# A split index projection and a three-block first product in a two-block transformer kernel

## The reference

```
for l in 0, 1:
    h    = rmsnorm(x) * g
    proj = h @ w_in[l]       # q,k,v of A, B, C (512 columns each), q_idx 256, k_idx 64, w_idx 4, gates 3072
    q_B, k_B, q_C, k_C, q_idx, k_idx = rope(...)
    A    = band attention;  B = differential attention
    C    = attention over the 64 keys that score highest by
           sum_h w_idx[q,h] * relu(q_idx[q,h] . k_idx)
    x   += (sum of gated up-projections of A, B, C) @ w_out[l]     # "out", two halves of 512 columns
    x   += cross attention over 256 memory tokens
    x   += (silu(h2 @ w_g) * (h2 @ w_u)) @ w_down                  # "gate_up" in 11 pieces, "down" in 22 chunks
```

## Time and profile before

| what | value |
|---|---|
| median of 3 runs | 1891.83 us (1890.23 to 1896.19) |
| the profiled execution's own time | 1890.31 us |
| its span, first to last instruction | 1888.4 us |
| mean granted TensorE clock in the span | 0.948 |
| PE busy | 1697.2 us, 90% |
| DVE, ACT, POOL busy | 858.2, 578.8, 93.2 us |
| moved by DMA | 388.39 MB |

### The profile page before, as it was taken

How to read it: one execution, slowest core, us unless ns; L and a number is a source line. 1 busy time by engine, 2 the same in 40 slices (tenths; PEclk the granted TensorE clock), 3 DMA queues, 4 the chain that set the end, 5 groups by cost and what they waited for, 6 DMA issues and landing times.

```text
span 1888.4 us, 26405 instructions
## 1 busy us (share of the span) xinstructions
PE 1697.2 (90%) x10618; PEld 1349.3 (71%) x10618; DVE 858.2 (45%) x1151; ACT 578.8 (31%) x869; POOL 93.2 (5%) x50
## 2 busy tenths in 40 slices
PE   6958799999999969999899799997999889979997
PEld 5836444444444349878788699997978778869997
DVE  1782301111011045367745376646446655366653
ACT  1030111111110134253521354433425451144442
POOL 0000000000000000125000000000016100000000
PEclk8978799999999989999999899998999999989998
DMA  9052299999999954324323255463423323345550
GB/s 337 1 222 89 104 430 428 428 428 429 428 429 429 427 199 162 129 95 142 127 90 134 89 182 188 167 238 119 165 93 134 130 94 115 109 133 184 175 200 23
DMA packets 121754, 388.39 MB, mean 206 GB/s; under 512 B 3504, under 2 KB 55088, under 8 KB 109360
## 3 DMA queue, kind: packets, MB, share of 16 engines
q1 hardware_dynamic: 121648, 386.91, 53.6%
HBM read 385.85 MB, written 1.05 MB: 205 GB/s over the span
## 4 chain that ended last, share of the span: by engine, by line
PE 67%; DVE 11%; DMA 9%; issue 6%; ACT 5%; POOL 1%; DVEq 0%; SPq 0%; ACTq 0%; POOLq 0%
PE psum L913 9%; DMA ring<-w 9%; PE psum L732 8%; PE psum L733 8%; PE psum L735 7%; PE psum L1097 4%; PE psum L722 4%; PE psum L935 3%; DVE outs L1454 3%; PE psum L1156 2%; PE psum L1159 2%; PE psum L1158 2%; PE psum L897 2%; PE psum L879 2%; ACT probs L1184 1%
## 5 line engine op out<-in xcount | busy, mean ns | idle before, releaser
L526 DVE TENSOR_TENSOR w_lo<-raw,w_hi 128x1024 fp32r<-128x1024 f32 x244 | 295.0, 1223 | 204.2 <-ACT w_hi L1187 201.6
L1187 ACT ACTIVATE w_hi<-raw 128x1024 fp32r<-128x1024 f32 x268 | 278.6, 1053 | 286.6 <-PE psum L735 104.2
L732 PE MATMUL psum<-h_hi,w_hi 128*128 128x256 f32 x1408 | 353.5, 288 | 7.5 <-DVE big L1682 7.5
L733 PE MATMUL psum<-h_hi,w_lo 128*128 128x256 f32 x1408 | 348.2, 285 | 0.0
L732 PEld LDWEIGHTS psum<-h_hi,w_hi 128*128 128x128 f32 x1408 | 272.5, 194 | 14.6 <-issue 14.0
L733 PEld LDWEIGHTS psum<-h_hi,w_lo 128*128 128x128 f32 x1408 | 272.6, 194 | 0.1
L913 PE MATMUL psum<-ring,outs 128*64 128x512 f32 x1024 | 232.7, 611 | 22.8 <-DMA ring<-w 21.4
L913 PEld LDWEIGHTS psum<-ring,outs 128*64 128x64 f32 x1024 | 81.4, 141 | 171.9 <-issue 171.9
L735 PE MATMUL psum<-h_lo,w_hi 128*128 128x256 f32 x1408 | 197.4, 283 | 0.0
L1615 DVE TENSOR_TENSOR qk<-big,psum 128x512 f32<-128x512 f32 x16 | 17.2, 1077 | 368.5 <-PE psum L913 368.5
L735 PEld LDWEIGHTS psum<-h_lo,w_hi 128*128 128x128 f32 x1408 | 181.6, 192 | 0.0
(11 more groups left out here) (239 smaller groups left out, 2282.4 us busy)
## 6 DMA issues: line engine op xcount, KB each, us to landing
ring<-w SPq DMA_DIRECT2D x96, 2048.0 KB, 16.4
raw<-w_in SPq DMA_DIRECT2D x30, 2048.0 KB, 7.9
raw<-w_gu SPq DMA_DIRECT2D x44, 1024.0 KB, 7.1
raw<-w_down SPq DMA_DIRECT2D x12, 1536.0 KB, 6.4
ring<-w_in SPq DMA_DIRECT2D x5, 2048.0 KB, 17.3
raw<-w_out SPq DMA_DIRECT2D x4, 2048.0 KB, 8.0
ring<-w_out SPq DMA_DIRECT2D x2, 2048.0 KB, 14.3
raw<-w_up_a SPq DMA_DIRECT2D x2, 2048.0 KB, 7.7
```

Source lines behind the costliest of these rows:

```text
L526: return eng.tensor_tensor(chunk_part(w_lo, n), chunk_raw(n), chunk_part(w_hi, n).bitcast(F32), ALU.subtract)
L732: mm(to, hi[:, k, :], h_hi[:, k, :], start=(k == 0), stop=False)
L733: mm(to, lo[:, k, :], h_hi[:, k, :], start=False, stop=False)
L1187: return nca.activation(out_ap, in_ap, ACT.Copy)
```

## The change

The index piece becomes a split piece of 384 columns in 3 chunks (the 60 columns past the 324 are the first ones of the gates and are not used). `index_proj` is three calls of `split_chunk`, with all output channels on the partitions. ACT copies q_idx, k_idx (twice) and the block with w_idx out in four instructions, the last into rows of the `score` tile. The index rope moves from before attention A into its second step, behind `scores 0` and `probs 0` and ahead of the first gate chunk. After its rotation PE turns w_idx around with two transposes, and DVE scales it and frees the tile `p_idx` there. Since the number of chunks is now 137, `BUFFER` gives each chunk's buffer, with one break at chunk 71, so that the buffers go on in turn from one layer to the next. `first_project` does three blocks by halves and the fourth block whole, after them.

```diff
-IDX = ("in", 4608, 324)
+IDX = ("in", 4608, 3 * P)
@@ is_split, chunks_of
-    return piece[0] in ("out", "gu", "down") or (piece[0] == "in" and piece[2] == HALF)
+    return piece[0] in ("out", "gu", "down", "in")
+    if piece == IDX:
+        return 3
+TURN = SPLIT_THROUGH[23]
+BUFFER = [(n if n < TURN else n - N_CHUNKS) % PARTS for n in range(N_CHUNKS)]
@@ WORK
-        + [("rope", 2, "idx")]
-        + attention(0, 8, gate_parts((1, 5), 7, 0))
+        + attention(0, 8, {**gate_parts((1, 5), 7, 0), 1: [("rope", 2, "idx"), ("gates", 7, 0, 0)]})
@@ with_splits
-        used += {"proj": 4, "proj_v": 4, "out": 4, "gate_up": 4, "gates": 1, "down": 1}.get(w[0], 0)
+        used += {"proj": 4, "proj_v": 4, "out": 4, "gate_up": 4, "gates": 1, "down": 1, "index_proj": 3}.get(w[0], 0)
@@ buffer_user
-            if n >= PARTS:
-                return n - PARTS
-            return next(j for j in range(N_CHUNKS - PARTS, N_CHUNKS) if j % PARTS == n) - N_CHUNKS
+            earlier = [j for j in range(n - N_CHUNKS, n) if BUFFER[j % N_CHUNKS] == BUFFER[n]]
+            return max(earlier)
@@ first_project (PE)
+                halves = [slice(0, 4), slice(4, KD)]
+
+                def products(o, ks, parts, h, last_k=None):
+                    for k in range(KD)[ks]:
+                        for part in parts:
+                            last = mm(to[:, o, :], chunk_part(part, chunk[o])[:, k, :], h[:, k, :],
+                                      start=(k == 0 and o % 2 == 0 and part is w_hi and h is h_hi),
+                                      stop=(k == last_k), skip_group_check=True)
+                    return last
+
                 pe.wait_ge(h_hi_ready, base + 1)
-                for o in range(4):
+                for o in range(3):
                     pe.wait_ge(w_hi_ready, l * N_CHUNKS + chunk[o] + 1)
...
+                    products(o, halves[0], [w_hi], h_hi)
+                for o in range(3):
                     parts_ready(pe, chunk[o], l)
...
+                    products(o, halves[0], [w_lo], h_hi)
                 pe.wait_ge(h_lo_ready, base + 1)
...
+                for o in range(3):
+                    products(o, halves[0], [w_hi], h_lo)
+                pe.wait_ge(h_hi_ready, base + 2)
+                for o in range(3):
+                    products(o, halves[1], [w_hi, w_lo], h_hi)
+                pe.wait_ge(h_lo_ready, base + 2)
+                for o in range(3):
+                    products(o, halves[1], [w_hi], h_lo, KD - 1).then_inc(chunk_used, 1)
                     if o == 1 and NORM_OF[i]:
                         layer_sums(NORM_OF[i], l)
+                parts_ready(pe, chunk[3], l)
+                products(3, slice(0, KD), [w_hi, w_lo], h_hi)
+                products(3, slice(0, KD), [w_hi], h_lo, KD - 1).then_inc(chunk_used, 1)
@@ index_proj (PE)
-                        raw_arrived(pe, i, l)
                         enter(pe, "p_idx", l)
...
+                        for o in range(3):
+                            split_chunk(w[1], o, duo("p_idx")[:, o * SEQ:(o + 1) * SEQ], l)
@@ rope (PE)
-                        freed(pe, f"p_{name}", l)
+                        if name == "idx":
+                            pe.wait_ge(idx_raw, l + 1)
+                        else:
+                            freed(pe, f"p_{name}", l)
...
+                        if name == "idx":
+                            for t in range(TT):
+                                last = pe.transpose(duo("p_idx")[:, 768 + 64 * t:832 + 64 * t],
+                                                    score[64:128, t * P:(t + 1) * P], ident[64:128, 64:128])
+                            last.then_inc(wi_turned, 1)
@@ index_proj (ACT)
-                        copy(qiT[:], view(duo("p_idx"), 0, 3, SEQ)).then_inc(idx_raw, 1)
+                        copy(qiT[:, 0:2, :], view(duo("p_idx"), 0, 2, SEQ))
+                        copy(qiT[0:64, 2, :], duo("p_idx")[0:64, 512:768])
+                        copy(qiT[64:128, 2, :], duo("p_idx")[0:64, 512:768])
+                        copy(score[64:128, :], duo("p_idx")[64:128, 512:768]).then_inc(idx_raw, 1)
@@ rope (DVE), at its end; index_proj on DVE is gone
+                        if name == "idx":
+                            v.wait_ge(wi_turned, l + 1)
+                            for t in range(TT):
+                                last = v.tensor_scalar(wi[:, t, :], duo("p_idx")[:, 768 + 64 * t:772 + 64 * t],
+                                                       tok_mix[:, t:t + 1], 0.5, ALU.mult, ALU.mult)
+                            last.then_inc(free_of("p_idx"), 1)
```

More of the change, by code:

```diff
@@ L212, in with_splits @@
             out.append(w)
-        if direct_left and w[0] in ("index_proj", "up", "cross_v", "cross_q", "cross_o"):
+        if direct_left and w[0] in ("up", "cross_v", "cross_q", "cross_o"):
             assert direct_left.pop(0) == w[1]
@@ L452, in build @@
          w2_done, ysb_ready, scat_done, scat_added, moe_chain,
-         lam_dot, lam_exp, rot_done, cos_ready, rope_ready, idx_raw, idx_done, relu_ready, selneg_ready,
+         lam_dot, lam_exp, rot_done, cos_ready, rope_ready, idx_raw, wi_turned, idx_done, relu_ready, selneg_ready,
          scores_done, rowmax_ready, exp_ready, probs_ready, probsT_done, probsT_ready, attn_done, subln_ready,
@@ L463, in build @@
             "w2_done ysb_ready scat_done scat_added moe_chain "
-            "lam_dot lam_exp rot_done cos_ready rope_ready idx_raw idx_done relu_ready selneg_ready "
+            "lam_dot lam_exp rot_done cos_ready rope_ready idx_raw wi_turned idx_done relu_ready selneg_ready "
             "scores_done rowmax_ready exp_ready probs_ready probsT_done probsT_ready attn_done subln_ready "
@@ L547, in chunk_raw @@
                 return view(raw_of(i), o * D, KD, P)
-            whole = view(raw_of(i), 0, KD, HALF)
+            whole = view(raw_of(i), 0, KD, LAYER_PIECES[i][2] if LAYER_PIECES[i] == IDX else HALF)
             return whole[:, 2 * o:2 * o + 2, :] if is_values(i) else whole[:, :, o * P:(o + 1) * P]
@@ L562, in chunk_part @@
             dims = (2, HALF) if is_values(i) else (KD, P)
-            return view(parts[:, n % PARTS, :], 0, *dims)
+            return view(parts[:, BUFFER[n], :], 0, *dims)
         def linker(eng, chain, per=0, index=0):
@@ L726, in split_chunk @@
             def split_chunk(i, o, to, l):
-                n = SPLIT_THROUGH[i] - 4 + o
+                n = SPLIT_THROUGH[i] - chunks_of(LAYER_PIECES[i]) + o
                 parts_ready(pe, n, l)
@@ L766, in first_project @@
+                for o in range(3):
                     parts_ready(pe, chunk[o], l)
-                    for k in range(4):
-                        mm(to[:, o, :], chunk_part(w_lo, chunk[o])[:, k, :], h_hi[:, k, :], start=False, stop=False,
-                           skip_group_check=True)
+                    products(o, halves[0], [w_lo], h_hi)
                 pe.wait_ge(h_lo_ready, base + 1)
[L771 to L787, removed]
+                for o in range(3):
+                    products(o, halves[0], [w_hi], h_lo)
@@ L981, in _ @@
                     elif kind == "index_proj":
-                        i = w[1]
-                        raw_arrived(pe, i, l)
                         enter(pe, "p_idx", l)
[L985 to L999, removed]
+                        for o in range(3):
+                            split_chunk(w[1], o, duo("p_idx")[:, o * SEQ:(o + 1) * SEQ], l)
                     elif kind == "rope":
                         r, name = w[1], w[2]
-                        freed(pe, f"p_{name}", l)
+                        if name == "idx":
+                            pe.wait_ge(idx_raw, l + 1)
+                        else:
+                            freed(pe, f"p_{name}", l)
                         enter(pe, f"r_{name}", l)
```

## The result

| | before | changed |
|---|---|---|
| median | 1891.03 us (1889.72 to 1896.19, 4 runs) | 1870.04 us (1869.63 to 1871.82, 4 runs) |
| span of the profiled execution | 1888.4 us | 1867.8 us |

The ratio is 0.9888, 95% interval 0.9870 to 0.9907: 21.0 us less, where 26.6 were forecast. First the list of PE's waits in the changed kernel (line, for whom, total us, times, longest). Line 766 is now every matmul of the first products, 747 the norm's sums, 996 the index rotation, 1035 the scores.

What follows compares the result with a forecast made beforehand. PE, busy 90%, bounds the kernel through its instructions, gaps and clock. Per layer index 9.7, mix 2.1, `out` 3.9, ffn -2.4, twice: 26.6 us off 1891.8 gives 1865.2 us; 8-in-10 range 1856 to 1876.

Steps and rivals of the forecast that it cites:

- index to second gate chunk: Index stage, from the index product to the second gate chunk: 27.14 to 17.5 us, a gain of 9.7 a layer.
- mix: First product of mix: waits of 0.7 and 2.7 us, one clock drop; gain 2.1 us a layer, bounds 0.3 and 3.8.
- `out`: First product of `out`: 16.63 to 12.75 us, 1.0 us wait, full clock; gain 3.9 us a layer, 2.2 if it drops.
- ffn: First product of ffn: wait moves to `h_lo`; loss 0.7 us, 2.4 with a clock drop; 2.4 a layer taken.
- the held multiply: DVE's multiply of unit 0's probabilities, held beside POOL's cosine: near 1.1 us in place of 0.42.
- scores 1 released by `wi`: Index stage: unit 1's scores wait for DVE's write of `wi`, which frees their PSUM tile; PE waits 1.5 us.
- one drop of 1.7 us: Mix: the clock falls once after the 2.7 us wait at the sums, costing 1.7 us as in `out` before.
- The wait that moves: Ffn: PE's wait for the weights' high part is not removed but moves to `h_lo`, 3.3 us, longer than before.
- Little from the waits: Rival: first products end with their late inputs at low clock, index gains only its matmuls; 16.2 us, 1875.6; chance 0.18.
- A did not go to the low clock: Rival: the index rope's gaps drop attention A to the low clock, up to 33 us more a layer; 1931; chance 0.03.
- The clock was not kept: Rival: the new waits of 2.7 and 3.3 us leave the clock full; gain 35 us, 1857; chance 0.17.

Runs made afterwards that it cites:

- e12: The changed kernel with the index scores' relu written back to PSUM, where DVE reads it; 1870.24 us against 1870.04.
- e2: The kernel before with only the new three-block `first_project`; 1890.41 us, ratio 0.9992.
- e3: The changed kernel with DVE writing both `h_lo` parts in ffn ahead of the fourth chunk's low part; 1864.41 us, ratio 0.9853.
- e6: The changed kernel with the index rope ahead of `probs 0` in DVE's queue; 1867.51 us, ratio 0.9871.

## Why the prediction was right, and where it was off

Times in us from PE's first matmul of one stretch to its first of the next; "forecast" is what the prediction took.

| step | before, layers 0 / 1 | forecast | changed, layers 0 / 1 |
|---|---|---|---|
| index to second gate chunk | 27.14 / 27.17 | 17.5 | 17.67 / 17.67 |
| mix | 21.01 / 21.04 | 18.9 | 20.46 / 20.47 |
| `out` | 16.62 / 16.61 | 12.75 | 12.80 / 12.80 |
| ffn | 14.59 / 14.62 | 17.0 | 17.36 / 18.00 |
| between `out` and ffn | 62.52 / 62.52 | no change | 63.86 / 63.18 |
| rest of attention A | 35.73 / 35.41 | no change | 36.01 / 35.99 |
| index scores to `out` | 167.01 / 167.31 | no change | 166.64 / 166.58 |

- *Index.* Right in size and by its steps: three chunks in 8.9 us against 8.64, copies until 788.0, 1.38 us of PE's wait against 1.3, the held multiply 1.46 us against 1.1, scores 1 released by `wi` after a wait of 1.18 us against 1.5. The hold beside POOL was 1.04 us long; with the rope ahead of the multiply the stage is 1.07 us shorter.
- *`out`.* Right: a wait of 0.85 us against 1.0, full clock.
- *Mix, the term that was mis-sized.* The waits were right (0.59 and 2.53 us against 0.7 and 2.7), the clock's price was not: one drop of 1.7 us was taken, 0.3 to 3.8 us of gain were the bounds, and 0.55 came in both layers, 3.1 us less than forecast. In the run with the first product alone the same instructions took 18.94 us after the same wait of 2.53 us, which is the forecast, and 17.42 where the wait was 1.9 us: about 3 us lie between the outcomes of one piece of code. The changed kernel had the longest of them in both layers, and so had e12; e2, e3 and e6 had the two shorter ones with the same code. What decides is open.
- *Ffn.* The wait that moves was right: 3.59 and 3.09 us against 3.3; the loss was 2.8 and 3.4 against 2.4, again by the clock (0.90 and 0.81). The prediction's own times give 0.6 us for the loss without the clock, not 0.7. Moving `h_lo` ahead took away wait and loss.
- *Not foreseen.* Between `out` and ffn 2.0 us were lost in both layers together, and 0.9 in attention A. The first model ended 1.0 us earlier, and index to `out` was 1.1 us shorter. Of these no cause was tested. Between `out` and ffn PE's waits have the same lengths in both kernels, to 0.5 us, and what differs is how long and where the clock was low (0.86 before, 0.84 and 0.89 after).
- *What the forecast had by luck.* It took the stretch from index to `out` as fixed. It is not: 166.6 to 172.5 us in the ten kernels that leave it alone. Had the changed kernel fallen into the pattern of the index part alone, it would have been some 7 us slower, 1877, just outside the range of 1856 to 1876.
- *The rivals.* "Little from the waits" (1875.6) was the nearer one: mix and ffn came out as it said, index and `out` did not. A did not go to the low clock (0.98). The clock was not kept.

## What to carry to other kernels

When a wait is taken out of an in-order queue, name the next input that is late, and look in the releasing engine's own list for something that needn't stand ahead of it: here three moves in the lists of DVE and PE together gave 17 us more. Judge an experiment on an interleaved kernel by the windows of the stretch that it touches, beside its total: a stretch after it can give back all that was saved, for a reason of its own. A chain on VectorE that PE will wait for is worth having one of its inputs in PSUM while GpSimd works; where PE doesn't wait for it, as in the changed kernel, it brought nothing. And where two profiles of the same code differ by 3 us in one stage, one profile of each kernel can't price an edit of 2 us.

## What the runs showed of the hardware

- The multiply-adds of the index score on DVE, with two inputs in SBUF, took 2.0 to 2.7 us when held and 0.35 or 0.48 (128 or 256 columns) otherwise. In the ten kernels that have them so, 87 of the 93 held ones began while a POOL instruction ran, and none of the 67 others did. With one input in PSUM all 64 of four kernels took 0.35 or 0.48 us, though 56 of them began while POOL ran. The Trainium skill, SBUF — State Buffer, section "Who interferes with whom", says that a VectorE instruction with two SBUF inputs contends with a GpSimd instruction that reads SBUF; these durations agree with it.
- How many of the eight were held in a layer (3, 4 or 6) differed between kernels, and between the two layers of one kernel, though their code is the same. Six came with the full clock at the start of the stretch, three or four with the low one, in 20 layers of 20.
- The first product mix took 20.46 or 18.9 us after one and the same wait of 2.53 us, and 17.4 after one of 1.9. From the sums to its end, 7.40, 5.89 and 4.33 us, the clock was 0.54, 0.71 and 1.00. Which of them came was not fixed by that code alone. With unused matmuls in the wait all four mixes took 17.45 to 17.74 us; of the ten without them two took 17.4 and the others 18.9 or more.
